# Between two transformer blocks: squares read from PSUM by halves, the residual in one operation, and the second block's turned tokens in four PSUM banks of their own

## The reference, cut to what matters

```python
def rms_norm(x, g):
    y = x * lax.rsqrt(jnp.mean(x * x, axis=-1, keepdims=True) + EPS)
    return y * g
# end of block 1
x1 = x + rms_norm(m @ w_o, norm_post)
# start of block 2
h = rmsnorm(x1, norm_attn) * (1 + sc_a) + sh_a
qa, ka, va, cq, ckv, kr = jnp.split(h @ w_in_2, SPLIT_POINTS, axis=-1)
# attention over keys of the context and of x1, w_out_2, a mixture of 16 experts, norm_final
```

## Time and profile before

| what | value |
|---|---|
| median of 3 runs | 705.34 us (704.82 to 707.81) |
| the profiled execution | 705.55 us, of which 703.7 us between the first and the last instruction |
| PE busy | 596.1 us, 85% of the span |
| DVE, ACT busy | 295.1 us, 224.1 us |
| data read | 190.9 MB, 273 GB/s over the span |

### The profile page before, as it was taken

How to read it: one execution, slowest core, us unless ns; L and a number is a source line. 1 busy time by engine, 2 the same in 40 slices (tenths; PEclk the granted TensorE clock), 3 DMA queues, 4 the chain that set the end, 5 groups by cost and what they waited for, 6 DMA issues and landing times.

```text
span 703.7 us, 8506 instructions
## 1 busy us (share of the span) xinstructions
PE 596.1 (85%) x3351; PEld 367.7 (52%) x3351; DVE 295.1 (42%) x725; ACT 224.1 (32%) x483; POOL 17.6 (3%) x34
## 2 busy tenths in 40 slices
PE   6989999999998979979998999977995775665663
PEld 6978886878676757648654444436430321221010
DVE  3365676666574252464728876145110100010005
ACT  4344454435344224365235666111010100010001
POOL 3000000000000001000000000000000000000000
PEclk9999999999999999999999999997998979898687
DMA  8595756777686790354475002754999999999992
GB/s 335 208 360 192 279 206 261 285 277 294 266 327 271 272 406 39 119 210 180 169 305 243 0 1 73 286 206 183 375 430 427 426 424 431 428 424 427 426 414 85
DMA packets 19080, 193.00 MB, mean 274 GB/s; under 512 B 3296, under 2 KB 4576, under 8 KB 7264
## 3 DMA queue, kind: packets, MB, share of 16 engines
q1 hardware_dynamic: 15584, 188.49, 66.6%
q10 hardware_dynamic: 3168, 2.39, 1.1%
q0 software_dynamic: 288, 1.57, 0.5%
HBM read 190.87 MB, written 1.05 MB: 273 GB/s over the span
## 4 chain that ended last, share of the span: by engine, by line
PE 63%; DMA 24%; DVE 7%; ACT 3%; issue 2%; POOL 0%; SPq 0%; ACTq 0%; POOLq 0%; DVEq 0%
PE bank L1017 25%; DMA qk<-in_stream 17%; PE bank L994 5%; PE bank L1005 5%; DMA ring<-in_stream 5%; PE bank L1523 3%; PE bank L1436 3%; PE bank L1282 3%; PE bank L1399 3%; PE bank L1367 2%; PE bank L1056 2%; PE bank L1364 2%; PE bank L1470 2%; PE bank L1309 2%; DMA vvc<-vvc 1%
## 5 line engine op out<-in xcount | busy, mean ns | idle before, releaser
L1017 PE MATMUL bank<-weight_parts,u_parts 128*128 128x512 f32 (+2 forms) x416 | 126.7, 387 | 3.7 <-ACT rows L654 1.2
L1752 DVE TENSOR_TENSOR weight_parts<-ring,weight_parts 128x1024 fp32r<-128x1024 f32 (+2 forms) x64 | 73.3, 1180 | 46.1 <-ACT weight_parts L654 44.0
L1017 PEld LDWEIGHTS bank<-weight_parts,u_parts 128*128 128x128 f32 x416 | 76.5, 190 | 21.2 <-issue 2.1
L654 ACT ACTIVATE weight_parts<-ring 128x1024 fp32r<-128x1024 f32 (+2 forms) x64 | 64.1, 1022 | 33.6 <-PE bank L1017 24.0
L1017 PE MATMUL bank<-weight_parts,x_parts 128*128 128x512 f32 (+1 forms) x128 | 48.3, 378 | 0.0
L994 PEld LDWEIGHTS bank<-ident,sp 128*128 128x128 f32 (+1 forms) x218 | 26.1, 140 | 24.8 <-DVE sp L2040 15.6
L1017 PE MATMUL bank<-u_parts,weight_parts 128*128 128x256 f32 x192 | 36.7, 288 | 2.2 <-DVE weight_parts L1752 2.2
L994 PE MATMUL bank<-ident,sp 128*128 128x128 f32 (+1 forms) x218 | 32.1, 274 | 3.5 <-DVE sp L2040 1.9
L705 ACT ACTIVATE sp<-sp,small 128x128 f32<-128x128 f32 (+1 forms) x48 | 21.3, 444 | 35.8 <-DVE small L1713 35.8
L1017 PEld LDWEIGHTS bank<-u_parts,weight_parts 128*128 128x128 f32 x192 | 30.4, 191 | 3.3 <-issue 2.2
L2145 DVE SCALAR_TENSOR_TENSOR sp<-sp,bank 128x512 f32<-128x512 f32 x4 | 2.8, 688 | 60.3 <-ACT sp L924 60.3
(11 more groups left out here) (292 smaller groups left out, 1032.6 us busy)
## 6 DMA issues: line engine op xcount, KB each, us to landing
ring<-in_stream SPq DMA_DIRECT2D x44, 2048.0 KB, 9.3
parts<-in_stream SPq DMA_DIRECT2D x12, 2048.0 KB, 35.0
qk<-in_stream SPq DMA_DIRECT2D x10, 2048.0 KB, 13.0
tabs<-in_stream SPq DMA_DIRECT2D x5, 2048.0 KB, 35.5
mo<-in_stream SPq DMA_DIRECT2D x5, 2048.0 KB, 38.7
vvc<-in_stream SPq DMA_DIRECT2D x5, 2048.0 KB, 37.6
tz<-in_stream SPq DMA_DIRECT2D x5, 1024.0 KB, 39.6
lat<-in_stream SPq DMA_DIRECT2D x5, 1024.0 KB, 41.7
```

The lines of the kernel that those rows point to most:

```text
L654: ins = act.activation(dst, src, ACT.Copy, scale=scale)
L1017: ins = pe_.matmul(o, lhs(a, c, i), rhs(b, c, i), start=(c == 0 and n == 0), stop=(c == chunks - 1 and n == 2))
L1752: dve.tensor_tensor(quarter(weight_parts[:, SLOT:], name, q), quarter(slot(name), name, q), quarter(weight_parts, name, q).bitcast(F32), A ...
```

## The change

- `hT00` to `hT11` take banks of their own (`ROUTER` gets four names), so the names left change the pairs in which they share banks 0 and 1.
- `DENSE` is reordered: `hT00 hT01` come straight behind `wo11`, then the four `ckv`, then `hT10 hT11`, and `xa02`; `kc0` to `kc3`, `modT2`, `bG` and `bF` are spread over the products behind it, up to `xa00`; `lq1` comes behind `xa10`.
- Of a `wo` half ACT no longer makes a copy: it squares the half straight from PSUM, and when that is done DVE multiplies the same half by the gain into `rn` and frees the bank (`post_gain`). The mean is put together from the two halves.
- The root and the residual are one operation for each half, `x + rn * root` ("residual"), and the squares of the sum are taken by halves too ("square").
- The residual, squares, means, normalising and the four quarters of X2 stand in a table `ACROSS`, by which they follow `wo01`, `wo11`, `ckv00` and `ckv01` on ACT and DVE.
- POOL takes its roots in the same order with other places; the counts of `squares` are named by a list.

The diff, without the hunks that only rename the counts of `squares`:

```diff
@@ -90,7 +90,7 @@
 WIDTH = {"W2": 280, "X2": 416}
-SPLIT_AFTER = {"hT01": "X2", "modT2": "X2", "bF1": "X2", "hT10": "X2"}
 
 DENSE = ["xT00", "xT01", "xT10", "xT11", "qa0", "qa1", "kvc", "kvs", "va0", "va1", "qb0", "qb1",
...
@@ -98,14 +98,14 @@
          "cO0", "cO1", "gA00", "gA10", "yaT0", "gA01", "yaT1", "gA11", "modT0", "wa00", "ybT0",
          "wa10", "ybT1", "wa01", "wa11", "gB00", "gB10", "cxT00", "cxT01", "cxT10", "cxT11",
          "gB01", "gB11", "wb00", "ck0", "wb10", "ck1", "wb01", "wb11", "mT00", "mT10", "mT01",
-         "mT11", "modT1", "wo00", "cc0", "cc1", "wo10", "clT", "wo01", "wo11", "ckv00", "ckv01",
-         "ckv10", "hT00", "hT01", "ckv11", "bG0", "bG1", "modT2", "bF1", "bF0", "hT10", "hT11",
-         "kc0", "kc1", "kc3", "xa02", "kc2", "xa12", "xa01", "xa11", "xa00", "lq0", "lq1",
-         "xa10", "lk0", "lk1", "qu00", "qu01", "xkv00", "xkv01", "qwT0", "qu10", "qwT1", "kwT",
+         "mT11", "modT1", "wo00", "cc0", "cc1", "wo10", "clT", "wo01", "wo11", "hT00", "hT01",
+         "ckv00", "ckv01", "ckv10", "ckv11", "hT10", "hT11", "xa02", "kc0", "xa12", "modT2", "kc1",
+         "xa01", "bG0", "bG1", "xa11", "kc2", "bF1", "kc3", "bF0", "xa00", "lq0",
+         "xa10", "lq1", "lk0", "lk1", "qu00", "qu01", "xkv00", "xkv01", "qwT0", "qu10", "qwT1", "kwT",
          "qu11", "xkv10", "xkv11", "qm0", "qm1", "qm2", "qm3", "kx0", "kx1", "kx2", "kx3"]
 TAIL = ["ou00", "ou01", "ou10", "rT00", "rT01", "ou11", "rT10", "rT11", "lg1", "ls1", "afT", "slT", "gx0", "gx1"]
-ROUTER = {"xT10": 2, "xT11": 3, "rT00": 2, "rT01": 3, "rT10": 4, "rT11": 5, "lg0": 6, "ls0": 7, "lg1": 6, "ls1": 7}
+ROUTER = {"hT00": 2, "hT01": 3, "hT10": 4, "hT11": 5, "xT10": 2, "xT11": 3, "rT00": 2, "rT01": 3, "rT10": 4, "rT11": 5, "lg0": 6, "ls0": 7, "lg1": 6, "ls1": 7}
 GROUPS = [name for name in DENSE + TAIL if name not in ROUTER]
 BANK_OF = {name: n % 2 for n, name in enumerate(GROUPS)} | ROUTER
 assert BANK_OF["gx0"] == 0 and BANK_OF["gx1"] == 1
...
@@ -128,20 +128,30 @@
     ["qb0", "qb1", "kb0", "kb1", "vb0", "vb1", "za0", "za1", "zb0", "zb1", "gA00", "gA10", "gA01", "gA11"])}
+X2_SPLIT = SPLIT.index("X2")
+ACROSS = {"wo01": [("high", 0), ("residual", 0), ("square", 0), ("high", 1), ("mean", 0), ("low", 0), ("norm", 0)],
+          "wo11": [("high", 2), ("low", 1), ("residual", 1)], "ckv00": [("square", 1), ("mean", 1), ("low", 2), ("norm", 1)],
+          "ckv01": [("high", 3), ("low", 3)]}
+SQUARES = ["x0", "x1", "wo00", "cc0", "cc1", "wo10", "wo01", "x00", "x01", "wo11", "x10", "x11", "q0", "kv0", "q1", "kv1",
+           "ou00", "ou01", "ou10", "ou11", "f00", "f01", "f10", "f11"]
+
+def squared(name):
+    return SQUARES.index(name) + 1
+
 def schedule():
     out = []
     for name in DENSE:
         for k in range(1, len(SPLIT)):
-            if LAST_USE[SPLIT[k - 1]] == name and SPLIT[k] not in SPLIT_AFTER.values():
+            if LAST_USE[SPLIT[k - 1]] == name and SPLIT[k] != "X2":
                 out += [("split", (k, q)) for q in range(4)]
         out.append(("dense", name))
         if name == "xT11":
             out += [("split", (0, q)) for q in range(4)]
-        if name in SPLIT_AFTER:
-            k = SPLIT.index(SPLIT_AFTER[name])
-            out.append(("split", (k, sum(i == ("split", (k, q)) for i in out for q in range(4)))))
+        out += ACROSS.get(name, [])
         if name in MOD_AFTER:
             out.append(("mod", MOD_AFTER[name]))
         if name in ROUND_AFTER:
...
@@ -695,6 +705,15 @@
                     if n:
                         quarter_released(eng, n - 1, q)
                     copy(quarter(weight_parts, name, q), quarter(slot(name), name, q)).then_inc(split_a, 1)
+                elif kind == "high":
+                    arrived(eng, "X2")
+                    quarter_released(eng, X2_SPLIT - 1, n)
+                    copy(quarter(weight_parts, "X2", n), quarter(slot("X2"), "X2", n)).then_inc(split_a, 1)
+                elif kind == "square":
+                    for h in range(2):
+                        eng.wait_ge(x1_ready, 2 * n + h + 1)
+                        sum_squares(xn[:, n, 512 * h:512 * h + 512], 10 + n if h else 8 + n, sp[:, 0:512])
                 elif kind == "score":
                     u = n
...
@@ -809,15 +828,7 @@
                     elif name[:2] == "wo":
                         filled(eng, name)
                         t, h = int(name[2]), int(name[3])
-                        copy(rn[:, t, 512 * h:512 * h + 512], D_(name)[:, :], name)
-                        if h == 1:
-                            kept(eng, f"wo{t}0")
-                            kept(eng, name)
-                            sum_squares(rn[:, t, :], 4 + t, sp[:, 0:D])
-                            if t == 0:
-
-                                eng.wait_ge(x1_ready, 1)
-                                sum_squares(xn[:, 0, :], 8, sp[:, 0:D])
+                        sum_squares(D_(name)[:, :], 14 + t if h else 4 + t, sp[:, 0:512])
                     elif name[:2] in ("bG", "bF"):
                         filled(eng, name)
...
@@ -855,9 +866,6 @@
                         src = D_(name)[:, :].rearrange("p (h d) -> p h d", h=4)
                         copy(kcat[:, tk, 4 * h:4 * h + 4, 0:NOPE], src[:, :, 0:64])
                         leave(copy(vm[:, tk, 4 * h:4 * h + 4, :], src[:, :, 64:128]), name)
-                        if name == "ckv11":
-                            eng.wait_ge(x1_ready, 2)
-                            sum_squares(xn[:, 1, :], 9, sp[:, 0:D])
                     elif name[:2] in ("qm", "kx", "kc") and int(name[2]) % 2 == 0:
                         filled(eng, name)
                         copy(mla_turned(name), D_(name)[0:QK, :].rearrange("p (h s) -> p h s", h=2), name)
...
@@ -954,7 +962,7 @@
             pool.memset(view(vc, 3520, 544), 0.0).then_inc(zeroed, 1)
             eng.wait_ge(zeroed, 1)
-            for n, (k, w) in enumerate([(0, 1), (1, 1), (2, 2), (6, 2), (4, 1), (8, 1), (5, 1), (9, 1), (10, 2), (12, 2),
+            for n, (k, w) in enumerate([(0, 1), (1, 1), (2, 2), (6, 2), (14, 1), (10, 1), (15, 1), (11, 1), (10, 2), (12, 2),
                                         (14, 1), (15, 1), (4, 1), (5, 1)]):
                 eng.wait_ge(means, n + 1)
                 pool.tensor_tensor(rs[:, k:k + w], ss[:, k:k + w], half[:, 2:3].to_broadcast([P, w]), ALU.pow)\
...
@@ -1626,13 +1634,21 @@
                 mean_root(k + t, 1, D, n_squares)
                 dve.tensor_scalar(dst[:, t, :], xn[:, t, :], rs[:, k + t:k + t + 1], None, ALU.mult).then_inc(normed, 1)
-            def block1_norm(t):
-
-                mean_root(4 + t, 1, D, 5 + 2 * t)
+            def post_gain(t, h):
+                name = f"wo{t}{h}"
+                filled(eng, name)
                 eng.wait_ge(post_in, 16)
-                own(dve.scalar_tensor_tensor(rn[:, t, :], rn[:, t, :], rs[:, 4 + t:5 + t], post, ALU.mult, ALU.mult))
-                dve.tensor_tensor(xn[:, t, :], xn[:, t, :], rn[:, t, :], ALU.add).then_inc(x1_ready, 1)
-                eng.wait_ge(x1_ready, t + 1)
+                cols = slice(512 * h, 512 * h + 512)
+                eng.wait_ge(squares, squared(name))
+                leave(dve.tensor_tensor(rn[:, t, cols], D_(name)[:, :], post[:, cols], ALU.mult), name)
+            def half_mean(k, k_first, n_squares):
+                eng.wait_ge(squares, n_squares)
+                dve.scalar_tensor_tensor(ss[:, k:k + 1], ss[:, k:k + 1], 1.0 / D, ss[:, k_first:k_first + 1],
+                                         ALU.mult, ALU.add).then_inc(means, 1)
+                n_mean[0] += 1
             def rotate(x, t, heads, n, at):
...
@@ -1751,6 +1767,24 @@
                     eng.wait_ge(split_a, 4 * n + q + 1)
                     dve.tensor_tensor(quarter(weight_parts[:, SLOT:], name, q), quarter(slot(name), name, q),
                                       quarter(weight_parts, name, q).bitcast(F32), ALU.subtract).then_inc(split_v, 1)
+                elif kind == "low":
+                    eng.wait_ge(split_a, 4 * X2_SPLIT + n + 1)
+                    dve.tensor_tensor(quarter(weight_parts[:, SLOT:], "X2", n), quarter(slot("X2"), "X2", n),
+                                      quarter(weight_parts, "X2", n).bitcast(F32), ALU.subtract).then_inc(split_v, 1)
+                elif kind == "residual":
+                    eng.wait_ge(roots, n_mean[0])
+                    for h in range(2):
+                        kept(eng, f"wo{n}{h}")
+                        x = xn[:, n, 512 * h:512 * h + 512]
+                        dve.scalar_tensor_tensor(x, rn[:, n, 512 * h:512 * h + 512], rs[:, 14 + n:15 + n], x, ALU.mult, ALU.add)\
+                           .then_inc(x1_ready, 1)
+                elif kind == "mean":
+                    first_half(8 + n, squared(f"x{n}0"))
+                    half_mean(10 + n, 8 + n, squared(f"x{n}1"))
+                elif kind == "norm":
+                    eng.wait_ge(roots, n_mean[0])
```

(17 more changed lines are left out.)

12 lines of the change are left out of this document (6 added, 6 removed).

## The result

The changed kernel takes 712.75 us, the median of 4 runs (711.60 to 713.44), and the kernel before took 705.32 (704.82 to 707.81) beside it: a ratio of 1.0092, 95% interval 1.0074 to 1.0110. So it is slower by 6.5 us by the ratio and by 7.4 us between the medians, where 1.4 was forecast, and the time lies above the range of 703.8 to 709.3.

The account below looks back on a forecast made before the run. TensorE's unbroken order up to the attention's last score bounds the kernel, since the experts' weight stream waits for it; the marker is `qu00`. -4.4, +6.4 - 0.2 and -0.4 give +1.4 us: 705.34 to 706.7 us, range 703.8 to 709.3.

Parts of the forecast that it names:

- step 1: From `clT` to `wo01`: DVE frees `wo10`'s bank only behind WO1's four low quarters; 1.4 us lost.
- step 2: From `wo01` to `hT00`: tile 0's norm chain ends after `wo11`; 0.9 us of new TensorE idle.
- step 3: From `hT00` to the end of `xa12`: almost no TensorE waits; 4.4 us won, the first two steps included.
- step 4: From `xa12`'s end to `xa00`: filling work between products waits behind ACT and DVE queues; 6.4 us idle, before 0.2.
- step 5: From `xa00` to `qu00`: `lq1` no longer waits for `late_x(1)`; 13.7 us for 14.1, 0.4 us won.
- The rival with both falls of the clock: Clock falls in new idle times ahead of `wo01` and `xa00`: both 709.9 us, chance 0.07; one 708.3, 0.25.
- The Trainium skill's rule: In the clock rival: small idle times between groups cycling through PSUM banks suffice to halve the clock; both stretches would pay.
- The owed waits stay hidden: Between `xa12` and `xa00`, ACT and DVE empty the shared banks in time: 701 us, half hidden 704; chance 0.12.
- X1 comes late: X1's load shares the transfer with X0's and lands 4.4 us later, delaying `xa01`: 711.0 us; chance 0.05.
- The change does not do what it says: X2's quarters, landing 2 us late, hold up tile 0's norm chain and `hT00`: 708.7 us; chance 0.03.

Follow-up runs that it names:

- e1: Changed kernel with unread identity products filling TensorE's idle times ahead of `wo01`, `bF1`, `kc3` and `xa00`: 709.52 us, 1.0045 of before.
- e2: Changed kernel with DVE's normalising and residual ahead of X2's low quarters, so no split runs beside a POOL root: 709.51 us, 1.0047 of before.
- e7: Changed kernel, same order, with 14 more names (filling work, `clT`, `lq`, `lk`) in banks apart from the two shared ones: 700.25 us, 0.9922 of before.
- e5: Changed kernel with a bank of its own for `wo01`: 709.62 us, 1.0068 of before.
- e3: Changed kernel with the filling work in one block behind `hT11` and ahead of `xa02`: 705.59 us, 0.9996 of before.
- e4: Changed kernel with the last quarter of WO1's split behind `wo10` instead of ahead of it: 709.42 us, 1.0047 of before.
- e8: Changed kernel with e7's banks, norm and residual ahead of low quarters, and filling work moved into the waits ahead of `hT00` and `hT10`: 695.49 us, 0.9851 of before.
- e10: Kernel before with only the four turned tokens' banks (`hT00` to `hT11`) added: 706.29 us, 1.0006 of before.
- e9: Kernel before, old order and norm, with e7's banks apart and the turned tokens' banks: 700.16 us, 0.9908 of before.
- e11: e7 with 14 unread identity products ahead of `hT00`: 701.27 us, 0.9909 of before.

## Why the prediction was wrong

The terms as they were forecast, at full clock (e1), and in the profile of after, in us:

| stretch | forecast | e1 | after |
|---|---|---|---|
| `clT` to `wo01` (step 1) | 3.20 | 3.17 | 3.17 |
| `wo01` to `hT00` (step 2) | 11.85 | 12.86 | 14.15 |
| `hT00` to `hT10` (step 3) | 8.10 | 8.91 | 8.92 |
| `hT10` to the end of `xa12` (step 3) | 10.80 | 10.91 | 10.91 |
| end of `xa12` to `xa00` (step 4) | 23.1 | 23.15 | 23.13 |
| `xa00` to `qu00` (step 5) | 13.7 | 13.97 | 15.75 |
| sum | 70.75 | 72.97 | 76.03 |

**Steps 1 and 4 were right.** DVE frees `wo10`'s bank behind the low quarters, and the second half owes what was said: at full clock, in e2, its waits up to `xa00` add up to 5.3 us (6.4 were forecast) and those behind to 1.1 (1.4), each with the releaser that was named, and the stretches from start to start are met within 0.3 us (the brackets add up to less than the starts lose, since matmuls that don't wait overlap). The text called them waits for places in an engine's order; e7 shows that what makes these places matter is the sharing of two banks.

**Two steps failed: the clock, which the sum put at nothing, and the root in step 2.**

**Step 2 mis-sized the root.** It took 0.56 us from the rows of before, where DVE stood idle and waited for POOL. The change puts a low quarter of X2 there to use that idle time, and beside it the root takes 1.27: DVE's work doesn't hide the root, it holds it up. DVE then waits 0.45, 0.44 and 0.44 us at three places where the layout had none. One of them lies in step 2 and two in the way to `hT10`, whose wait (0.96 for 0) is nearly that. This is 1.3 of the 2.2 us by which e1 misses the forecast. Another 0.5 is the rest of step 2: in e1 `wo01` takes 5.62 us from its start to that of `wo11`, where 5.46 was laid out, the squares of the sum end 0.1 later behind the start of the residual, and the handovers from there to the end of the normalising take 0.2 more. The remaining 0.4 is 0.3 in step 5 (13.97 for 13.7), whose waits are no longer than forecast, so that it was TensorE's own work that was laid out too short, and 0.1 ahead of the end of `xa12`. Little of the roots' part was had back by putting the quarters behind: e2 won 0.3.

**The rival with both falls of the clock is what happened, and it had 0.07.** It was priced at 3.2 us and measures 3.06. What failed is the weighing: the sum counted full clock, and the falls were left to a rival. Its chance rested on one stretch of before that kept 1.00 with 2.36 of 5.20 us busy, against one that didn't with 2.88 of 5.40, so I took one fall at 0.25 and both at 0.07. Here both stretches fell in both profiles of this kernel, while e2 and e5, with waits as long or longer, kept 1.00 in theirs. Counted over the profiles with unfilled waits: behind the 2.57 us ahead of `wo01` the clock fell in three of four (after twice, e3; not e2), behind a wait of 2.67 to 3.51 us ahead of `hT00` in two of three (e4, e7; not e5), and in the waits from `bF1` to `xa00` in two of five (after twice; not e2, e4, e5). So one stretch that kept 1.00 was no ground for a small chance. Even odds for each new long wait would have been the better reading, and a range up to 712. The Trainium skill's rule (TensorE: Matmul & The Clock Gate, A second HAM failure mode), cited against the change, agrees with after and not with e2.

**The sum.** The forecast column is 70.75 - 69.46 = 1.29 over before, which the prediction rounded to 1.4. With the roots and small terms (2.22) and the two falls (3.06) it becomes 6.57, which is what was measured. The medians differ by 7.4 us because the profiled execution of after is the shortest of its four, 1.15 under their median, and that of before 0.23 over its own: 6.05 + 1.15 + 0.23 = 7.43. The fall at `wo00`, 1.1 us of the 6.05, is in three of the thirteen profiles (before, e8, e10).

**The other rivals.** "The owed waits stay hidden" did not come, and its sentence from the Trainium skill (Perfetto Trace Analysis, Matmuls), that groups should rotate through PSUM banks, agrees with these runs only once the filling work rotates too: the four banks alone give 1.0006 (e10), with 14 more names apart it is 0.9908 (e9). "X1 comes late" didn't come either: in after ACT's first quarter of X1 (312.56) waits for PE's last use of the parts and not for the transfer, and in e7, where it does wait for the transfer, TensorE doesn't. "The change does not do what it says" named the right chain and the wrong delay: it had X2's quarters late by their landing, and what they cost was DVE's low quarter beside the roots, which none of the rivals had.

## What to carry to other kernels

Groups that share two banks tie TensorE to the slowest entry in the queues that empty them, so before moving filling work between products, look whether spare banks can take it: here the banks alone were worth 6 us (e9), and reordering without them cost up to 7. The time in which DVE waits for a small operation on POOL isn't a free slot for a large DVE operation with two SBUF inputs: put that one behind the operation that waits for POOL, and look at what it then holds up. And when a change trades short waits for fewer, longer ones on TensorE, price the fall of the clock in the likeliest case and not in a far rival, then measure its price by filling the wait with products that nobody reads.

## What the runs showed of the hardware

- A POOL operation on 128x1 takes 0.56 us alone and 1.26 to 1.27 beside a DVE operation of 1.02 us that started 0.16 us ahead of it; it ends 0.4 us behind DVE's end (six of six cases in the two profiles of the changed kernel). With the DVE operation moved behind, it is 0.55 or 0.56 again (e2).
- Behind waits of TensorE of 2.57 us, and of 1.29 and 0.48 us with one product between, the granted clock went to 0.50 in after (1.2 GHz), at a cost of 1.3 and 1.8 us. Behind the same waits it stayed at 1.00 in e2. Behind a wait of 3.45 us (e5) it stayed at 1.00, behind 3.51 (e7) it was 0.78 over the next 6 us. Every fall in this stretch came behind waits like these; what decides whether it comes, these runs leave open.
- With the waits filled by unread products the clock was 1.00 in both kernels where it was tried, in one profile of each, and the stretch was shorter by 3.1 us (e1 beside after) and 0.5 us (e11 beside e7).
